# A top-k search with its state in PSUM, index-score relus in place in PSUM, and a later place for the second low half of the MLP hidden pair

## What is computed

```
def sq_relu_ffn(h, w1, w2):
    return jnp.square(jax.nn.relu(h @ w1)) @ w2          # 1024 -> 4096 -> 1024

# dsa_attend, the index scores and the selection
qk_idx = einsum('bqhe,bke->bqhk', qi, ki) * (D_IDX ** -0.5)           # 4 index heads of 64
score = einsum('bqhk,bqh->bqk', relu(qk_idx), wi) * (H_IDX ** -0.5)
score = where(admissible, score, NEG)
_, idx = lax.top_k(score, top_k)                          # 256 keys (136 for the sample rows)
```

## Time and profile before

| what | value |
|---|---|
| median of 3 runs | 2800.72 us (2800.42 to 2802.06) |
| the profiled execution, its own time | 2799.82 us |
| its span in the profile | 2798.1 us |
| TensorE busy | 2654.0 us (95%) |
| VectorE busy | 1242.0 us (44%) |
| ScalarE busy | 667.4 us (24%) |
| GpSimd busy | 1166.8 us (42%) |
| mean granted TensorE clock | 0.973 |

### The profile page before, as it was taken

How to read it: one execution, slowest core, us unless ns; L and a number is a source line. 1 busy time by engine, 2 the same in 40 slices (tenths; PEclk the granted TensorE clock), 3 DMA queues, 4 the chain that set the end, 5 groups by cost and what they waited for, 6 DMA issues and landing times.

```text
span 2798.1 us, 38333 instructions
## 1 busy us (share of the span) xinstructions
PE 2654.0 (95%) x16253; PEld 2448.9 (88%) x16253; DVE 1242.0 (44%) x1575; ACT 667.4 (24%) x926; POOL 1166.8 (42%) x969
## 2 busy tenths in 40 slices
PE   6999999999999999999978996899999999999998
PEld 6998744699999999999965995568999999999998
DVE  5223477634333232323348998464342323232334
ACT  3200378612010101000126751354110000000000
POOL 4332366444333333334433333772433334444441
PEclk8999999999999999999999998799999999999999
DMA  5110300011111111111012110301111111111101
GB/s 189 46 46 32 114 9 1 38 57 45 45 45 45 45 45 45 45 45 45 20 66 69 45 45 15 65 2 63 46 46 45 45 45 45 45 45 45 45 30 63
DMA packets 96239, 134.02 MB, mean 48 GB/s; under 512 B 17393, under 2 KB 81969, under 8 KB 95634
## 3 DMA queue, kind: packets, MB, share of 16 engines
q1 hardware_dynamic: 92466, 114.35, 12.9%
q10 hardware_dynamic: 3680, 18.36, 1.6%
HBM read 113.16 MB, written 18.73 MB: 47 GB/s over the span
## 4 chain that ended last, share of the span: by engine, by line
PE 75%; DVE 12%; ACT 6%; issue 3%; POOL 2%; DMA 1%; another core or an unknown queue 0%; DVEq 0%; ACTq 0%; POOLq 0%
PE PS L259 63%; ACT reach L1242 3%; PE PS L1211 2%; PE PS L1184 2%; DVE xT L347 1%; PE PS L1153 1%; DVE rbuf L336 1%; ACT rbuf L316 1%; ACT hid L318 1%; PE PS L868 1%; PE PS L896 1%; DVE score L1312 1%; POOL spr L1015 1%; DVE reach L1340 1%; DVE sp L971 1%
## 5 line engine op out<-in xcount | busy, mean ns | idle before, releaser
L1676 POOL TENSOR_TENSOR w_sp<-stage,ones 128x512 fp32r<-128x512 f32 x372 | 391.9, 1086 | 1403.7 <-PE PS L259 1363.7
L259 PE MATMUL PS<-h,w_sp 128*128 128x352 f32 (+1 forms) x5256 | 873.4, 326 | 42.8 <-POOL w_sp L1680 14.7
L259 PEld LDWEIGHTS PS<-h,w_sp 128*128 128x128 f32 (+1 forms) x5256 | 856.1, 189 | 51.8 <-issue 25.3
L259 PE MATMUL PS<-hid,w_sp 128*128 128x352 f32 x4608 | 756.4, 324 | 19.6 <-DVE xT L347 19.6
L259 PEld LDWEIGHTS PS<-hid,w_sp 128*128 128x128 f32 x4608 | 743.4, 188 | 28.3 <-DVE xT L347 28.3
L259 PE MATMUL PS<-hz,w_sp 128*128 128x352 f32 x3456 | 567.7, 323 | 0.0
L259 PEld LDWEIGHTS PS<-hz,w_sp 128*128 128x128 f32 x3456 | 558.7, 188 | 0.0
L1680 POOL TENSOR_TENSOR w_sp<-stage,w_sp 128x512 fp32r<-128x512 f32 x372 | 526.5, 1449 | 0.0
L347 DVE TENSOR_TENSOR xT<-PS,xT 128x1056 f32<-128x1056 f32 x256 | 318.8, 1254 | 336.3 <-PE PS L259 336.3
L316 ACT ACTIVATE rbuf<-rbuf 128x1056 f32<-128x1056 f32 x64 | 69.7, 1089 | 1259.3 <-DVE rbuf L336 1259.3
L336 DVE SCALAR_TENSOR_TENSOR rbuf<-PS,rstd 128x1056 f32<-128x1056 f32 x64 | 80.5, 1257 | 505.3 <-PE PS L259 505.3
(11 more groups left out here) (259 smaller groups left out, 1898.5 us busy)
## 6 DMA issues: line engine op xcount, KB each, us to landing
stage<-in_w_ffn SPq DMA_DIRECT2D x64, 1024.0 KB, 5.1
stage<-in_w_in_odd SPq DMA_DIRECT2D x10, 1024.0 KB, 4.9
stage<-in_w_in_even SPq DMA_DIRECT2D x9, 1024.0 KB, 5.0
x_spill<-xT ACTq DMA_DIRECT2D x2, 4224.0 KB, 14.0
xT<-x_spill ACTq DMA_DIRECT2D x2, 4224.0 KB, 13.5
xtok<-in_x_prompt SPq DMA_DIRECT2D x8, 512.0 KB, 7.7
stage<-in_w_out_even SPq DMA_DIRECT2D x4, 1024.0 KB, 8.9
stage<-in_w_out_odd SPq DMA_DIRECT2D x4, 1024.0 KB, 13.4
```

The costliest lines, as they stand in the source:

```text
L259: mm = pe.matmul(out[0:m, c, :], lhs, rhs(k, b)[:, c * CH:(c + 1) * CH], start=(k == 0 and n == 0), stop=(k == nk - 1 and n == 2))
L1676: pool.tensor_tensor(w_sp[:, s, 0, q:q + 512], stage[:, s, q:q + 512], ones[:, 0:1].to_broadcast([P, 512]), ALU.mult).then_inc(w_hi_done, 1)
```

## The change

There are three edits. In the MLP, VectorE's low half of the second up job (t=1) is written after the first down job's addition, and no longer before it; chunk 0 keeps the old order. In the index scores ScalarE writes the relu back to the PSUM banks that it read, VectorE accumulates from there, and the two `rl` buffers are gone; with them goes ScalarE's wait for the accumulation, and TensorE's two waits now ask for accumulations (four pairs back in the loop, the 27th of 28 before the projection) in place of relus. In the search the rows `KV`, `KEPT` and `THR` of the state move to PSUM bank 7; `UP` is made from `THR` with another bit mask where it was made from the candidate; and one copy of `THR` back to SBUF follows the rounds.

```diff
--- before.py
+++ after.py
@@ -327,33 +327,38 @@
             dve.wait_ge(rt_done, 3 * times)
             ch.link(dve.reciprocal(rstd[:, :], rstd[:, :]))
 
-            def up(c, dj2=0, dj=0, dt=0):
+            def low(c, t, dt=0):
+                dve.wait_ge(hhi_done, c0 + 2 * c + t + 1 + dt)
+                dve.tensor_tensor(hid[:, c % 2, t, 1, :], rbuf[:, t, :], hid[:, c % 2, t, 0, :].bitcast(F32),
+                                  ALU.subtract).then_inc(hid_ready, 1)
+
+            def up(c, dj2=0, dj=0, dt=0, last=True):
                 j = j0 if c == 0 else j0 + 2 + 10 * (c - 1)
                 for t in range(2):
-                    n = c0 + 2 * c + t
                     dve.wait_ge(job_done, j + t + 1 + dj)
 
                     dve.scalar_tensor_tensor(tri3(rbuf[:, t, :]), psz(j + t), 0.0, tri3(rstd[:, :]), ALU.max,
                                              ALU.mult).then_inc(set_free[(j + t) % 2], 1)
-                    dve.wait_ge(hhi_done, n + 1 + dt)
-                    dve.tensor_tensor(hid[:, c % 2, t, 1, :], rbuf[:, t, :], hid[:, c % 2, t, 0, :].bitcast(F32),
-                                      ALU.subtract).then_inc(hid_ready, 1)
-
-            def down(c, dj2=0, dj=0):
+                    if t == 0 or last:
+                        low(c, t, dt)
+
+            def down(c, dj2=0, dj=0, dt=0, low_of=None):
 
                 j = j0 + 2 + 10 * c + (2 if c < 15 else 0)
                 for m in range(KT):
                     dve.wait_ge(job_done, j + m + 1 + dj)
                     dve.tensor_tensor(tri3(xT[:, m, :]), psz(j + m), tri3(xT[:, m, :]),
                                       ALU.add).then_inc(set_free[(j + m) % 2], 1)
+                    if m == 0 and low_of is not None:
+                        low(low_of, 1, dt)
 
             up(0)
             with dve.Fori(0, 7) as i:
                 for c in (0, 1):
-                    up(c + 1, dj2=i * 10, dj=i * 20, dt=i * 4)
-                    down(c, dj2=i * 10, dj=i * 20)
-            up(15)
-            down(14)
+                    up(c + 1, dj2=i * 10, dj=i * 20, dt=i * 4, last=False)
+                    down(c, dj2=i * 10, dj=i * 20, dt=i * 4, low_of=c + 1)
+            up(15, last=False)
+            down(14, low_of=15)
             down(15)
 
 
@@ -1029,7 +1034,6 @@
         yc = at("yc", o_z + OC * ZB, [P, NT + 2])
         ytap = at("ytap", o_z + (OC + 2) * ZB, [P, NT + 2])
         zslot = lambda name, s, shape: at(name, o_z + s * ZB, shape)
-        rl = [zslot("rl0", 9, [P, D]), zslot("rl1", 10, [P, D])]
         qiP = zslot("qiP", 16, [P, 4, NT])
         kiD = zslot("kiD", 11, [P, NT])
         kipT = zslot("kipT", 12, [P, PAST])
@@ -1096,7 +1100,7 @@
             for n in range(28):
...
                 if n >= 4:
-                    pe.wait_ge(i_relu, n - 3)
+                    pe.wait_ge(i_acc, n - 3)
                 b0 = 2 * (n % 4)
                 if bi < 6:
                     b = bi + 2
@@ -1109,7 +1113,7 @@
                     pe.matmul(PS[0:TS, b0, :], q, kipT[:, :], start=True, stop=True)
                     mm = pe.matmul(PS[0:TS, b0 + 1, 0:TS], q, kiD[:, TP:NT], start=True, stop=True)
                 mm.then_inc(i_mm, 1)
-            pe.wait_ge(i_relu, 28)
+            pe.wait_ge(i_acc, 27)
             with pe.Fori(0, 4) as i:
                 for s in range(2):
                     gemm_in_unit(pe, U_OIN + 2 + s, J_OIN + 2 * s, du=i * 2, dj2=i * 2)
@@ -1226,11 +1230,8 @@
             for n in range(28):
                 bi = n // 4
                 act.wait_ge(i_mm, n + 1)
-                if n >= 2:
-                    act.wait_ge(i_acc, n - 1)
-                m = ROWS[bi]
-                act.activation(rl[n % 2][0:m, 0:SCN[bi]], banks(2 * (n % 4), SCN[bi], m), ACT.Relu,
-                               scale=HD * HD ** -0.5).then_inc(i_relu, 1)
+                x = banks(2 * (n % 4), SCN[bi], ROWS[bi])
+                act.activation(x, x, ACT.Relu, scale=HD * HD ** -0.5).then_inc(i_relu, 1)
             act.wait_ge(i_acc, 28)
             act.wait_ge(ki_out, 32)
 
@@ -1303,7 +1304,7 @@
                 m = ROWS[bi]
                 tile = bi + 2 if bi < 6 else 8
                 s = score[0:m, SC0[bi]:SC0[bi] + SCN[bi]]
-                x, w = rl[n % 2][0:m, 0:SCN[bi]], wi[0:m, tile, hh:hh + 1]
+                x, w = banks(2 * (n % 4), SCN[bi], m), wi[0:m, tile, hh:hh + 1]
                 dve.wait_ge(i_relu, n + 1)
                 if hh == 0:
                     dve.tensor_scalar(s, x, w, None, ALU.mult).then_inc(i_acc, 1)
@@ -1322,13 +1323,16 @@
             CNT, KV, KEPT, THR, UP, LOW = range(2, 8)
             f = lambda r, a=0, b=7: bs_[:, r, a:b]
             u = lambda r, a=0, b=7: bs_[:, r, a:b].bitcast(I32)
+            state = PS[:, 7, 0:64].rearrange("p (r b) -> p r b", b=8)
+            fp = lambda r: state[:, r, 0:7]
+            up_ = lambda r: state[:, r, 0:7].bitcast(I32)
             dve.wait_ge(i_acc, 28)
             ch.mark(dve.memset(f(CNT), 0.0))
-            ch.mark(dve.memset(u(THR), -1))
+            ch.mark(dve.memset(up_(THR), -1))
             for bi in range(7):
                 n, k = SCN[bi], TOPK if bi < 6 else TOPK_S
 
-                ch.mark(dve.memset(bs_[:, KV, bi:bi + 1], float(n - 2 * k + 1 if bi in ACT_BLOCKS else n - k)))
+                ch.mark(dve.memset(state[:, KV, bi:bi + 1], float(n - 2 * k + 1 if bi in ACT_BLOCKS else n - k)))
             dve.memset(u(0), 0).then_inc(cand_set, 1)
             ch.sync()
 
@@ -1341,14 +1345,18 @@
                                               ALU.is_lt, ALU.add, accum_out=bs_[0:m, CNT, bi:bi + 1]))
                 if n < 31:
                     bit = 1 << (30 - n)
-                    ch.mark(dve.tensor_scalar(u(UP), u(now), bit, None, ALU.bitwise_xor))
-                    ch.mark(dve.tensor_scalar(u(nxt), u(THR), bit, None, ALU.bitwise_xor))
+                    if n == 0:
+                        ch.mark(dve.tensor_scalar(u(UP), u(now), bit, None, ALU.bitwise_xor))
+                    else:
+                        ch.mark(dve.tensor_scalar(u(UP), up_(THR), 3 * bit, None, ALU.bitwise_xor))
+                    ch.mark(dve.tensor_scalar(u(nxt), up_(THR), bit, None, ALU.bitwise_xor))
                 ch.sync()
                 dve.wait_ge(act_count, 3 * n + 3)
-                ch.link(dve.tensor_tensor(u(KEPT), f(CNT), f(KV), ALU.is_le))
+                ch.link(dve.tensor_tensor(up_(KEPT), f(CNT), fp(KV), ALU.is_le))
                 if n < 31:
-                    dve.copy_predicated(u(nxt), u(KEPT), u(UP)).then_inc(cand_set, 1)
-                ch.link(dve.copy_predicated(u(THR), u(KEPT), u(now)))
+                    dve.copy_predicated(u(nxt), up_(KEPT), u(UP)).then_inc(cand_set, 1)
+                ch.link(dve.copy_predicated(up_(THR), up_(KEPT), u(now)))
+            ch.link(dve.tensor_copy(u(THR), up_(THR)))
 
             LO16, HI16, SIGN, CARRY, STEP = LOW, UP, CNT, 1, KEPT
             ch.mark(dve.memset(u(THR)[32:64, 6:7], 0))
```

## The result

The changed kernel took 2769.12 us (median of 4 runs, 2766.6 to 2770.4) beside 2801.12 us for the kernel before on the same chips: a ratio of 0.9887, 95% interval 0.9872 to 0.9901, 32.0 us less. The forecast was 2769.1 us. Its profiled execution took 2769.18 us. Lines after 329 have moved: 336 is now 340, 339 is 332, 347 is 350, 1106 is 1110, 1232 is 1234, 1242 is 1243, 1253 is 1254, 1260 is 1261, 1309 is 1310, 1312 is 1313, 1348 is 1355, 1350 is 1357, 1351 is 1358, 1676 is 1684, 1680 is 1688.

What follows compares the result with a forecast made beforehand. TensorE's gemm line was taken to carry most of the chain, with stalls inside the MLPs. Gains of 27.3 (MLP) and 4.3 us (selection) sum to 31.6, giving 2769.1 us; range 2765 to 2777.5.

Steps and rivals of the forecast that it cites:

- the index term: Index scores: with relus in PSUM TensorE sets the pace, so scores and projection start come 3.8 us earlier.
- MLP, 27.3 us forecast: Both MLPs: reordering the low half removes 30 stalls of 0.91 us each, priced by whole periods.
- (a): MLPs: the stalls give back only their idle part, 19.6 us, for 2776.8 us; chance 0.10.
- 31.1: Index scores, a sign: projection's first matmul comes 31.1 us after the fourth relu's start, rather than 34.9.
- (b): Second mixer: a PSUM operand does not keep VectorE out of GpSimd's way; about 4 us lost, 2773.1 us; chance 0.08.
- Search, 0.5 us forecast: Search: its end keeps TensorE's pace; only a few small steps before GpSimd's unit ends gain, some 0.5 us.
- half or more was forecast: Search, a sign: ScalarE's evacuations (line 1253) now wait for TensorE in half of their cases or more.
- at most 0.56: Search: it was 0.56 us behind TensorE, so beyond the projection's earlier start its end gains no more than that.
- (d): Search: it runs free, as if ScalarE never waited for a job; 17 us more gain, 2752 us; chance 0.02.
- (c): Search state steps: PSUM writes cost up to 150 ns, adding 1.4 us, for 2770.5 us; chance 0.14.
- (e): MLPs: the late low half delays the second addition, moving the stall to the fourth down job; 2782.8 us; chance 0.03.
- (f): MLPs: TensorE without pauses gets a lower clock, making it slower, 2811 us at 0.97; chance 0.02.

Runs made afterwards that it cites:

- Experiment 1: Only the MLP edit, against the kernel before: 2774.22 us, ratio 0.9908.
- experiment 2: Only the index edit (relus in place in PSUM, TensorE waiting for accumulations), against the kernel before: 2795.58 us, ratio 0.9985.
- experiment 7: The changed kernel with an evacuation after every three search rounds and the search's state back in SBUF: 2763.99 us, ratio 0.9871 to the kernel before.
- Experiment 5: The kernel before with four relu buffers in SBUF instead of two, ScalarE waiting for the accumulation four back: 2799.39 us, ratio 1.0001.
- experiment 3: Only the search's state (`KV`, `KEPT`, `THR`) moved to PSUM, against the kernel before: 2800.82 us, ratio 1.0003.
- experiment 4: The changed kernel with the search's state back in SBUF, MLP and index edits kept: 2769.79 us, ratio 0.9889 to the kernel before.
- experiment 6: The changed kernel with an evacuation after every three search rounds instead of two and three in turn: 2746.98 us, ratio 0.9809 to the kernel before.

## Why the prediction was right

The mechanisms came as forecast; the agreement to 0.02 us is chance. The four runs of the changed kernel spread over 3.8 us, the index term was 0.5 us too large, and two stretches without an edit moved by +1.4 and -1.5 us and cancelled. By the stretches the gain is 30.6 us, by the medians 32.0, and 31.6 was forecast.

**MLP, 27.3 us forecast, 27.0 measured.** The step that mattered was to price the stall by the period (0.91 us) and not by the idle row (0.65). Experiment 1 excludes (a). The period of a chunk lost 0.90 us. The row of the weight loads' waits had nearly that price: 28.3 us in 30 waits, 0.94 us each, where the matmuls' idle row had 19.6. How the 0.25 us beyond the idle time divide between the weight load and the rest was not tried.

**Index scores, 3.8 us forecast, 3.3 measured in the stretch (3.7 us by experiment 2's medians).** Mechanism as forecast: matmuls run in one piece from 1463.76 and VectorE follows. The projection came 31.22 us after the fourth relu, where the prediction has 31.1. The term was 0.5 us too large. The 20 pairs took 25.82 us as worked out (fourth relu at 1469.26, last 128-row relu at 1495.08), but the fourth relu came 5.50 us after the first index matmul and not 5.09 as before: TensorE needed 1.29 us for a fourth narrow pair too, like for the first three, where before it took 0.87 for the fourth. TensorE had waited for a transfer ahead of the first pair, and both kernels begin the pairs with a granted clock of 0.50, the 1.2 GHz level; by the windows below it rose to 1.00 about 4.5 us after the first index matmul before, and 5.4 us after it in the changed kernel. From the windows around the fourth pair, before and after (columns as in the earlier trace rows):

```profile
1478.90:1480.20 1.30, 1.30 (x3) 0.68 (x3) 0.87 (x1) 0.51 (x2) 1.21 (x2) 0.50 0.98 291
1480.20:1482.00 1.80, 1.80 (x5) 0.76 (x4) 1.53 (x3) 1.01 (x3) 1.80 (x2) 0.95 1.12 336
```

```profile
1466.80:1468.10 1.30, 1.30 (x3) 0.67 (x2) 0.62 (x1) 0.49 (x2) 1.30 (x2) 0.50 0.98 299
1468.10:1470.00 1.90, 1.90 (x5) 0.85 (x4) 0.85 (x2) 0.82 (x2) 1.90 (x3) 0.73 1.12 330
```

This does not belong to the change: over the ten traces the fourth relu starts 4.90 to 5.50 us after the first index matmul, the later the later the clock rose, and with the index edit both ends occur (4.90 in experiment 7, 5.50 here). The index stretch is 36.1 to 36.8 us in the six traces with this edit. Rival (b) fell with the 1017 ns of 768 columns, beside a busy GpSimd. GpSimd gained as well: the same sixteen instructions beside the scores took 24.8 us before (1478.99 to 1503.75) and 17.9 us in the changed kernel (1466.77 to 1484.62). Experiment 5 shows that the operand's place did it, not the number of buffers.

**Search, 0.5 us forecast, 0.4 measured (-0.7 and +0.3).** The long steps are gone and ScalarE waits 15.9 us for jobs. The list names this wait at 5 of 12 evacuations, and half or more was forecast; the groups of three rounds between them took 11.63 us (1535.63 to 1547.26) where 11.42 is their own time, so they too were held, by 0.2 us. The search stretch became 0.7 us shorter, where "at most 0.56" was forecast. Experiments 3 and 4 show an edit without measurable worth. (d), the free search, fell with experiment 3; most of its 17 us came with experiment 6, by another order and still at the jobs' pace.

**Writes to PSUM (c).** Forecast 0 between -50 and +150 ns; measured -16 ns for the relu of 1024 columns and about +4 ns for the comparison. The Trainium skill ("Perfetto Trace Analysis", Optimizing Scalar/DVE Operations) has 125 ns for VectorE on PSUM beside 60 on SBUF; no step here shows the 65 ns, and the measurement decides. For ScalarE the Trainium skill has PSUM as the cheaper side in the same place (51 against 93 ns); the relu, whose output alone moved, agrees in sign, with 16 of the 42 ns.

**(e) and (f).** The second addition came in time, but with less cover than worked out: the low half took up to 2369 ns, not 1733, as it now starts at another moment of GpSimd's unit. The second addition ended at 699.15 where the fourth job's banks were needed at about 700.2: 1.0 us and not 1.5. The mean clock was 0.973 before and after, and PEclk is 1.00 over both MLPs in both kernels, so the pauses had bought none.

## What to carry to other kernels

Price a stall by the difference of whole periods; the idle row leaves out the restart. Look also at the waits of the weight loads. Before you count stalls as gain, look for an engine that is busy 100% beside them, and for the place where the stalled one waits for it: there the gain ends, and a change of the order in which they meet may be worth more than the repair (15 us of search against 0.7). And an edit tested alone with no effect may be the one that makes the next edit work: without state in PSUM the new order brought 6 us, with it 22.

## What was not expected of the hardware

Two stretches without any edit differ from execution to execution by up to 2.3 and 4.0 us. A good part of the second lies at the start of the sparse attention: the first 31 copies into `pT` took 48.3 us in experiment 1, whose stretch was the shortest, and 52.4 in experiment 4, whose stretch was the longest. All ten traces have a pause there, in which first one and then another engine stands with nothing to wait for that the profile shows. In the kernel before it was ScalarE, for 9.89 us, in the changed kernel VectorE, for 7.70 us. That pause alone does not explain the spread: TensorE's longest idle time in it was 7.6 us in the kernel before, but 5.6 in experiment 4. What it is was not tried.

```profile
1796.76 0.38 ACT L1287 ACTIVATE pT<-PS 128x256 f32<-128x256 f32 x1 [9.89 <-remote]
```

```profile
1781.32 0.42 DVE L1288 COPY pT<-PS 128x256 f32<-128x256 f32 x1 [7.70 <-remote]
```

The other is that the duration of a VectorE step with two SBUF operands depends on when in GpSimd's unit it starts: the low half of the second up job took 1.66 us in most chunks of the kernel before (at most 1733 ns), starting 0.5 us into an instruction of GpSimd; 2.35 to 2.37 us behind the first addition, where it starts 0.04 us after one; and 1.25 us behind the fifth, when GpSimd's unit is over. The instructions on both engines were the same.
